# Scores of the last 16 keys computed once for all heads, ahead of the attention steps

## The chip, the cores and the metric

The kernel runs on one core of a Trainium2 chip. The metric is the device time of one execution in microseconds. The core has TensorE (matrix products into PSUM), VectorE, ScalarE, GpSimd and SyncE (which here only issues transfers); each works through its own list of instructions in order, and they meet through semaphores. All data are 32-bit floats.

## The reference, cut to what matters

The reference is one step of a decoder layer: a normalised input of 528 prompt tokens (16 learned meta tokens and 512 others) and 8 sample tokens, one combined input projection, four mixers side by side (differential attention, retention, a gated recurrence, gated linear attention), gates and a merge, an output projection, and a mixture of experts. The change touches the prompt part of the attention:

```python
def diff_attn_block(q, k, v, q_pos, k_pos, lam):
    s = jnp.einsum('bqhmd,bkhmd->bhmqk', q, k)
    s = jnp.where(k_pos[None, :] <= q_pos[:, None], s, -jnp.inf)
    p = jax.nn.softmax(s, axis=-1)
    w = p[:, :, 0] - lam * p[:, :, 1]
    return jnp.einsum('bhqk,bkhv->bqhv', w.astype(v.dtype), v)
```

There are 4 heads `h`, and each has two maps `m` of width 32; the weights of a head are the difference of its two softmax maps.

## The kernel before, in words

TensorE computes the input projection tile by tile (`tiled`, `values_tile`): a tile is 128 output columns for all tokens, and it is made in two halves of about 3.7 us. The work of the mixers is laid between these halves: `beside(name, 0)` runs between the halves of tile `name`, and `beside(name, 1)` behind it. Each engine has a `beside` of its own or a loop in the same order. The order is written out by hand in the table `ATTN`: BK0 (behind) has step 0, BK1 1 and 2, BG0 3 and 4, BG1 5 and 6, V2 7 and 8, V3 9 and 10, CX0 11 and 12, CX1 13 and 14, CG0 15 and 16, CG1 17.

An attention step `s` belongs to a head and a block `i` of 128 queries: `head_block(s)` gives `(s // 8 * 2 + s % 2, s % 8 // 2)`. Queries of block `i` see 16 + 128 (i + 1) keys, so steps 6, 7, 14 and 15 (i = 3) have 528 keys. One PSUM bank holds 512 columns. The stages of a step are:

- `scores(s)` on TensorE (L681): for both maps the product into bank 4 + m, and for i = 3 the last 16 keys into bank 7 at column 256 + 16 m.
- `causal_max(s)` on VectorE (L1816 to L1824): it adds the mask in PSUM, takes the maximum, and for i = 3 does both for the last keys too and takes the smaller of the negated maxima (L1824).
- `exps(s)` on ScalarE (L1399, and L1403 for the last keys): exponentials with their sums, into `prb` in SBUF.
- `combine(s)` on VectorE (L1834 to L1838): the weights of the head, in `prb`; it ends with `scomb`.
- `transposes(s)` on TensorE (L699) into bank 6, and for i = 3 the fifth block into bank 7; `wt_copy(s)` on ScalarE (L1412, L1415) copies them to SBUF.
- `weighted(p)` on TensorE (L714): the output product of the step pair 2p and 2p + 1, into bank 7 at column 384; `av_copy(p)` on ScalarE (L1420) copies it.

`attention_step(s)` normally issues `weighted` (at odd s), `scores(s)` and `transposes(s - 1)`. Before the change the transposes of steps 6 and 14 are not issued in steps 7 and 15 but at the start of steps 8 and 16, and three waits keep bank 7 in order: the scores of a 528-key step wait for the output copy, and `weighted` and `transposes` wait for the exponentials of the last keys (`sexp`).

VectorE's list between these stages holds a rotation in steps 6, 8, 10 and 12 (`ROTATE`, L1844 to L1846) and key reductions of the sample attention (`K_BESIDE`, L1866), one in step 6, none in step 7, one each in 8, 14, 15 and 16. The products for these reductions are GpSimd's units (L2556); each of the first 15 waits for `scomb` at the step in `K_STEP`: unit 5 for the weights of step 6, unit 10 for those of step 14. SyncE loads the key pages for them in turn with the weight tiles of the projection.

Ahead of step 0, between the halves of BK0, TensorE transposes the sample columns of queries and keys (L801) into bank 4; ScalarE copies them (L1439) and sends them to a scratch in HBM, from which SyncE broadcasts them for GpSimd. Step 0 waits for that copy (`t8_ev`).

## Time and profile before

| | |
|---|---|
| median of 3 runs | 810.36 us (809.93 to 811.4) |
| the profiled execution's own time | 807.98 us |
| its span | 806.1 us, 14317 instructions |
| TensorE busy | 767.2 us |
| VectorE busy | 381.6 us |
| ScalarE busy | 223.3 us |
| GpSimd busy | 294.8 us |

The span is the time from the first to the last instruction of the profiled execution. Busy times of the engines overlap. L12 is line 12 of the kernel. A product of 32-bit floats is recorded as two matmul records (two passes), so a step with four products shows as x8. Where an instruction has waited, the idle time before it and the instruction that ended it stand in brackets.

### The profile page before, as it was taken

The page shows a single profiled execution, that of the slowest core. Times are in us where ns is not written, and L with a number is a line of the kernel's source. Part 1 is how long each engine was busy: PE and PEld are TensorE (multiplying, and loading weights), DVE is VectorE, ACT ScalarE, POOL GpSimd, SP SyncE. Part 2 cuts the span into 40 slices and gives each one's busy share as a digit, 9 for nine tenths or more (in the row PEclk, how much of TensorE's full clock was granted, in tenths as well). Part 3 has the DMA queues.
Part 4 walks back from the last instruction along what each step waited for, and adds up shares of the span by engine and source line. Part 5 has one row for each costly group of instructions (what it writes and reads, how often), then busy time and mean ns, then how long its engine had stood idle before and what let it go on. Part 6 is the DMA issues. An engine that isn't in the chain of part 4 may idle for free.

```text
span 806.1 us, 14317 instructions
## 1 busy us (share of the span) xinstructions
PE 767.2 (95%) x5269; PEld 549.3 (68%) x5269; DVE 381.6 (47%) x729; ACT 223.3 (28%) x432; POOL 294.8 (37%) x221
## 2 busy tenths in 40 slices
PE   9999999989999999999999999999999799999992
PEld 7887777666667878777777787888888544333330
DVE  4672586867469669653542211744433632030210
ACT  4231433331413535214413222521211521020100
POOL 0000422244653975335444554524332031333214
PEclk9999999999999999999999999999999999999997
DMA  9242842244654542155543454261580889999943
GB/s 365 106 156 84 241 140 80 89 137 155 170 188 162 184 142 92 37 162 170 170 146 96 154 170 158 65 223 69 201 320 1 311 289 411 378 387 373 381 149 49
DMA packets 72538, 148.32 MB, mean 184 GB/s; under 512 B 13335, under 2 KB 47144, under 8 KB 70420
## 3 DMA queue, kind: packets, MB, share of 16 engines
q1 hardware_dynamic: 65716, 135.43, 48.1%
q0 software_dynamic: 5920, 10.82, 5.3%
q10 hardware_dynamic: 832, 1.16, 0.6%
q8 instruction: 42, 0.69, 0.3%
q14 instruction: 28, 0.23, 0.1%
HBM read 137.71 MB, written 18.90 MB: 194 GB/s over the span
## 4 chain that ended last, share of the span: by engine, by line
PE 79%; DVE 10%; ACT 3%; DMA 2%; issue 2%; SPq 2%; ACTq 0%; POOL 0%; POOLq 0%; DVEq 0%
PE ps L879 18%; PE ps L606 13%; PE ps L1212 10%; PE ps L848 6%; PE ps L1120 6%; PE ps L1282 4%; PE ps L621 3%; PE ps L649 3%; PE ps L905 2%; PE ps L681 1%; PE ps L1201 1%; PE ps L595 1%; DMA out_y<-cst,gtab 1%; SPq L432 1%; PE ps L952 1%
## 5 line engine op out<-in xcount | busy, mean ns | idle before, releaser
L606 PE MATMUL ps<-xn,ring 128*128 128x268 f32 (+1 forms) x576 | 136.7, 392 | 0.2 <-ACT qk L1375 0.2
L606 PEld LDWEIGHTS ps<-xn,ring 128*128 128x128 f32 x576 | 106.9, 190 | 24.6 <-issue 3.9
L2556 POOL TENSOR_TENSOR kv<-kv,sgd 128x1024 f32<-128x1024 f32 (+1 forms) x32 | 79.8, 2507 | 114.4 <-DVE tmp L1838 64.7
L1532 ACT ACTIVATE sgt<-sgt,vec 128x260 f32<-128x260 f32 x60 | 30.1, 510 | 129.1 <-DVE sgt L2111 77.9
L2671 POOL DMA_INDIRECT out_y<-cst,gtab x24 | 37.3, 1555 | 74.6 <-DMA out_y<-cst,gtab 35.4
L848 PE MATMUL ps<-br,ring 128*128 128x260 f32 x256 | 61.2, 386 | 0.8 <-DVE sgt L2115 0.8
L879 PE MATMUL ps<-xn,ring 128*128 128x260 f32 x240 | 58.0, 384 | 1.0 <-ACT tmp L1375 1.0
L879 PE MATMUL ps<-xn,qb 128*128 128x260 f32 x240 | 57.6, 383 | 1.1 <-DVE sgt L2112 1.1
L848 PEld LDWEIGHTS ps<-br,ring 128*128 128x128 f32 x256 | 47.8, 190 | 11.8 <-issue 3.7
L879 PEld LDWEIGHTS ps<-xn,qb 128*128 128x128 f32 x240 | 45.4, 190 | 8.4 <-issue 1.4
L879 PEld LDWEIGHTS ps<-xn,ring 128*128 128x128 f32 x240 | 45.0, 190 | 8.3 <-issue 1.4
L1866 DVE TENSOR_REDUCE sgd<-kv 128x32 f32<-128x1024 f32 (+1 forms) x32 | 40.7, 1280 | 14.5 <-POOL kv L2556 14.5
L2468 DVE TENSOR_TENSOR ring<-ring,ps 128x256 f32<-128x256 f32 x12 | 5.1, 421 | 71.1 <-ACT ring L1691 69.9
L2102 DVE TENSOR_TENSOR sgt<-ps,sgt 128x260 f32<-128x260 f32 x15 | 6.4, 427 | 64.2 <-PE ps L879 64.2
L2600 POOL TENSOR_TENSOR qb<-qb,ring 128x512 f32<-128x512 f32 x15 | 19.3, 1287 | 41.2 <-PE ps L879 41.2
L2595 POOL TENSOR_TENSOR qb<-ring 128x512 f32<-128x512 f32 x15 | 20.5, 1364 | 36.6 <-PE ps L879 36.3
L2567 POOL TENSOR_TENSOR cst<-sgt,cst 128x520 f32<-128x520 f32 x16 | 20.6, 1289 | 30.6 <-ACTq L1542 30.6
L621 PE MATMUL ps<-kv,ring 128*128 128x268 f32 x128 | 29.8, 391 | 0.2 <-DVE kv L1751 0.2
L2607 POOL TENSOR_TENSOR qb<-ring,qb 128x512 f32<-128x512 f32 x15 | 19.3, 1287 | 28.9 <-PE ps L879 28.3
L649 PE MATMUL ps<-ring,xn 128*128 128x128 f32 x256 | 29.8, 276 | 0.0
L1375 ACT ACTIVATE cst<-ps 128x520 f32<-128x520 f32 x32 | 19.3, 603 | 37.5 <-PE ps L848 37.5
L649 PEld LDWEIGHTS ps<-ring,xn 128*128 128x128 f32 x256 | 29.1, 192 | 0.5 <-ACT tmp L1375 0.3
(516 smaller groups left out, 1505.6 us busy)
## 6 DMA issues: line engine op xcount, KB each, us to landing
ring<-in_w_mg SPq DMA_DIRECT2D x32, 640.0 KB, 4.6
kv<-in_kc SPq DMA_DIRECT2D x128, 128.0 KB, 2.1
kv<-in_vc SPq DMA_DIRECT2D x128, 128.0 KB, 2.1
ring<-in_w_in SPq DMA_DIRECT2D x24, 512.0 KB, 4.8
kv<-in_w SPq DMA_DIRECT2D x8, 1024.0 KB
br<-in_w SPq DMA_DIRECT2D x7, 1024.0 KB
sgd<-in_w SPq DMA_DIRECT2D x6, 1024.0 KB, 13.9
qk<-in_w SPq DMA_DIRECT2D x6, 1024.0 KB
```

Source lines behind the costliest of these rows:

```text
L606: mm = pe.matmul(ps[:, 2 * (t % 2) + h, 0:hw], wsl(c, k), xnv[:, k, col0 + h * hw:col0 + (h + 1) * hw], start=(k == 0), stop=(k == KT - 1))
L621: mm = pe.matmul(ps[:, EARLY[name] + h, 0:HT], wsl(c, k), xgv[:, k, h * HT:(h + 1) * HT], start=(k == 0), stop=(k == KT - 1))
L649: pe.matmul(ps[:, 2 * (t % 2), b * P:(b + 1) * P], xnv[:, k, b * P:(b + 1) * P], wsl(c, k), start=(k == 0), stop=(k == KT - 1))
L848: mm = pe.matmul(ps[:, bk + h, 0:HN], wsl(CAT[f"G{n}{m}"], KT + k), brv[:, BR[n] + k, h * HN:(h + 1) * HN], start=(k == 0), stop=(k == 1))
L879: mm = pe.matmul(ps[:, bk, 0:HN], w[:, k * P:(k + 1) * P], x, start=(k == 0), stop=(k == 3))
L1120: mm = pe.matmul(ps[:, bk, 0:HN], wk, x, start=(k == 0 and i in (1, 2, 5)), stop=(k == 3), skip_group_check=(i in (6, 7, 4, 3)))
L1212: mm = pe.matmul(ps[rows, i % ROUNDS, :], xeT[i % (2 * ROUNDS)][:, k, rows], slot[(i // ROUNDS * 12 + k - k % 2 + g // 2) % STREAM][2 * (g ...
L1282: mm = pe.matmul(ps[rows, LAST_OUT[r][n] if last else 6 + n, :], hT[r][:, f, rows], w[g][2 * f + n], start=(f == 0), stop=(f == 1), tile_p ...
L1532: act.activation(g, g, ACT.Sigmoid, bias=vv(V_BM + 8 * "ABCD".index(n) + m + i)).then_inc(g_a, 1)
L1866: dve.tensor_reduce(row, kb.rearrange("p s (m d) -> p s m d", d=32), X, ALU.add).then_inc(k_used, 1)
L2556: pool.tensor_tensor(kb, kb, qbc[:, b:b + 1, :].to_broadcast([P, HALF // 2 + (half and u), 256]), ALU.mult)\
L2671: pool.indirect_dma_start(out=o["y"], out_offset=on_rows(to), in_=rows.rearrange("p a n -> p (a n)"), in_offset=None, bounds_check=N - 1, ...
```

## The change

The scores of the last 16 keys are needed by the last query block of each head and map only. They are now computed once, for all 8 maps, between the halves of BK0: eight products into banks 4 to 7, columns 0 to 31, one bank for each group of 32 rows. VectorE (`last_keys`) adds the mask, writes them into `last_s` in SBUF and keeps their negated maxima in `last_m`. The sample transposes move to columns 256 to 511 of banks 4 and 5, and ScalarE's copy waits for VectorE's masking; step 0 waits for both. The steps with 528 keys compute 512 columns of scores, take one maximum in PSUM and combine it with `last_m`, and exponentiate the last keys from SBUF. The waits around bank 7 go, the first map's exponentials no longer wait for the second map's maximum, and the transposes of steps 6 and 14 stand in steps 7 and 15, behind the scores, like those of all other steps.

The pieces are, in order: the view, TensorE's `scores`, `transposes`, `weighted`, `attention_step` and `beside`, ScalarE's `exps` and `beside`, VectorE's `causal_max` and the new `last_keys`. ScalarE's `attention_step` has the same edit for `wt_copy` as TensorE's has for `transposes`.

```diff
+        last_s, last_m = view(sgt, 600, 4, 2, META), view(sgt, 600 + 8 * META, 4, 2)
...
             def scores(s):
...
-                if n > 512:
-                    pe.wait_ge(sav_ev, (s - 1) // 2)
+                k = min(n, 512)
                 for m in range(2):
                     r = slice(32 * ((2 * h + m) % 4), 32 * ((2 * h + m) % 4) + 32)
-                    for a, b, bk, at in ((0, min(n, 512), 4 + m, 0), (512, n, 7, 256 + META * m)):
-                        if a < b:
-                            if bk == 7 and m:
-                                pe.wait_ge(sco, 2 * s + 1)
-                            mm = pe.matmul(ps[:, bk, at:at + b - a], aqk[r, h // 2, META + P * i:META + P * (i + 1)],
-                                           aqk[r, 2 + h // 2, a:b], start=True, stop=True)
-                    mm.then_inc(sco, 1)
+                    pe.matmul(ps[:, 4 + m, 0:k], aqk[r, h // 2, META + P * i:META + P * (i + 1)], aqk[r, 2 + h // 2, 0:k],
+                              start=True, stop=True).then_inc(sco, 1)
...
             def transposes(s):
...
                 if i == 3:
                     pe.wait_ge(sav_ev, s // 2)
-                    pe.wait_ge(sexp, 4 * (s // 2) + 4)
...
             def weighted(p):
...
-                if i == 2:
-                    pe.wait_ge(sexp, 4 * p + 6)
...
             def attention_step(s):
-                if s in (8, 16):
-                    transposes(s - 2)
                 if 0 <= s < 16:
                     if s == 0:
-                        pe.wait_ge(t8_ev, 1)
+                        pe.wait_ge(t8_ev, 2)
                     scores(s)
-                if 1 <= s < 17 and s not in (7, 15):
+                if 1 <= s < 17:
                     transposes(s - 1)
...
                 if (name, end) == ("BK0", 0):
                     pe.wait_ge(a_ok, 4)
+                    for j in range(2):
+                        for g in range(4):
+                            r = slice(32 * g, 32 * g + 32)
+                            pe.matmul(ps[:, 4 + g, META * j:META * (j + 1)], aqk[r, j, L - P:L], aqk[r, 2 + j, 4 * P:L], start=True, stop=True)
                     for i in range(4):
-                        mm = pe.transpose(ps[0:DEC, 4, i * P:(i + 1) * P], aqk[:, i, L:T], ident)
+                        mm = pe.transpose(ps[0:DEC, 4 + i // 2, 256 + i % 2 * P:256 + (i % 2 + 1) * P], aqk[:, i, L:T], ident)
...
                 for m in range(2):
-                    act.wait_ge(smx, 2 * s + (2 if i == 3 else m + 1))
+                    act.wait_ge(smx, 2 * s + m + 1)
...
-                        ins = act.activation(prb[:, s % 2, m, 512:n], ps[:, 7, c0:c0 + META], ACT.Exp, bias=nb,
+                        ins = act.activation(prb[:, s % 2, m, 512:n], last_s[:, (2 * h + m) % 4, h // 2, :], ACT.Exp, bias=nb,
...
                 if (name, end) == ("BK0", 0):
                     act.wait_ge(t8, 1)
-                    link(act.activation(qk8, ps[0:DEC, 4, :], ACT.Copy))
+                    act.wait_ge(t8_ev, 1)
+                    link(act.activation(fold(qk8, 256), ps[0:DEC, 4:6, 256:512], ACT.Copy))
...
                     else:
-                        dve.wait_ge(sco, 2 * s + 2)
-                        link(tt(last, last, cc(C_MASK + P, META), ALU.add))
-                        dve.tensor_reduce(sc[:, 38:39], main, X, ALU.max, negate=True)
-                        link(dve.tensor_reduce(sc[:, 39:40], last, X, ALU.max, negate=True))
-                        tt(nb, sc[:, 38:39], sc[:, 39:40], ALU.min).then_inc(smx, 1)
+                        link(dve.tensor_reduce(sc[:, 38:39], main, X, ALU.max, negate=True))
+                        tt(nb, sc[:, 38:39], last_m[:, (2 * h + m) % 4, h // 2:h // 2 + 1], ALU.min).then_inc(smx, 1)
...
+            def last_keys():
+
+                dve.wait_ge(t8, 1)
+                link(tt(last_s, ps[:, 4:8, 0:2 * META].rearrange("p g (j k) -> p g j k", j=2),
+                        cc(C_MASK + P, META).unsqueeze(1).unsqueeze(1).to_broadcast([P, 4, 2, META]), ALU.add))
+                dve.sem_inc(t8_ev, 1)
+                link(dve.tensor_reduce(last_m, last_s, X, ALU.max, negate=True))
+
+            last_keys()
             at_k = 0
             for s in range(18):
```

## Rows read from the trace of the kernel before

**Rows 1.** The page: busy us, share of the span and instructions, by engine.

```profile
PE 767.2 (95%) x5269; PEld 549.3 (68%) x5269; DVE 381.6 (47%) x729; ACT 223.3 (28%) x432; POOL 294.8 (37%) x221
```

**Rows 2.** One stretch: busy PE, PEld, DVE, ACT, POOL; PEclk, DMA share, GB/s.

```profile
215.00:320.00 105.00, 103.45 (x586) 81.92 (x585) 77.75 (x91) 41.65 (x57) 62.79 (x51) 1.00 0.50 158
```

**Rows 3.** TensorE's timeline, steps 5 to 9: start, duration, instructions, [idle before].

```profile
105.93 0.94 PE L681 MATMUL ps<-qk 32*128 32x400 f32 x4
...
111.00 1.70 PE L681 MATMUL ps<-qk 32*128 32x512 f32 x8
112.63 0.66 PE L699 MATMUL ps<-cst,tmp 128*128 128x128 f32 x4
...
117.62 1.24 PE L714 MATMUL ps<-tmp,vtok 128*64 128x128 f32 x16 [0.76 <-ACT tmp L1403]
119.32 1.67 PE L681 MATMUL ps<-qk 32*128 32x512 f32 x8 [0.47 <-ACT br L1420]
120.92 3.84 PE L649 MATMUL ps<-ring,xn 128*128 128x128 f32 x32
124.69 0.65 PE L655 MATMUL ps<-ring,xn 128*32 128x128 f32 x16
126.56 0.74 PE L699 MATMUL ps<-cst,tmp 128*128 128x128 f32 x5 [1.22 <-ACT tmp L1403]
...
128.39 0.77 PE L699 MATMUL ps<-cst,tmp 128*128 128x128 f32 x5 [0.65 <-DVE tmp L1838]
128.99 3.74 PE L649 MATMUL ps<-ring,xn 128*128 128x128 f32 x32
...
134.05 0.52 PE L681 MATMUL ps<-qk 32*128 32x144 f32 x4
```

**Rows 4.** VectorE's timeline, steps 6 and 7.

```profile
112.29 0.30 DVE L1816 TENSOR_TENSOR ps<-ps,cst 128x128 f32<-128x128 f32 x1 [0.84 <-PE ps L681]
112.81 0.18 DVE L1821 TENSOR_TENSOR ps<-ps,cst 128x16 f32<-128x16 f32 x1 [0.22 <-PE ps L681]
...
113.63 0.16 DVE L1823 TENSOR_REDUCE small<-ps 128x1 f32<-128x16 f32 x1
...
115.33 0.71 DVE L1844 TENSOR_TENSOR qb<-qb,cst 128x536 f32<-128x536 f32 x1
...
118.60 0.15 DVE L1834 TENSOR_TENSOR small<-small 128x2 f32<-128x2 f32 x1
...
119.71 0.77 DVE L1838 SCALAR_TENSOR_TENSOR tmp<-tmp,small 128x528 f32<-128x528 f32 x1
...
122.12 0.81 DVE L1824 TENSOR_TENSOR small<-small 128x1 f32<-128x1 f32 x1
```

**Rows 5.** ScalarE's timeline, the exponentials of step 7.

```profile
124.45 0.69 ACT L1399 ACTIVATE tmp<-ps,small 128x512 f32<-128x512 f32 x1 [5.28 <-DVE small L1824]
...
126.04 0.28 ACT L1403 ACTIVATE tmp<-ps,small 128x16 f32<-128x16 f32 x1
```

**Rows 6.** GpSimd's timeline, its unit beside step 7.

```profile
120.56 2.36 POOL L2556 TENSOR_TENSOR kv<-kv,sgd 128x1024 f32<-128x1024 f32 x1 [12.86 <-DVE tmp L1838]
```

**Rows 7.** TensorE's timeline, steps 14 to 17.

```profile
161.78 1.70 PE L681 MATMUL ps<-qk 32*128 32x512 f32 x8
...
176.69 0.74 PE L699 MATMUL ps<-cst,tmp 128*128 128x128 f32 x5 [1.10 <-ACT tmp L1403]
178.52 0.77 PE L699 MATMUL ps<-cst,tmp 128*128 128x128 f32 x5 [1.10 <-DVE tmp L1838]
179.12 3.78 PE L606 MATMUL ps<-xn,ring 128*128 128x268 f32 x16
```

**Rows 8.** TensorE's timeline, the first attention step.

```profile
80.98 0.51 PE L681 MATMUL ps<-qk 32*128 32x144 f32 x4
```

**Rows 9.** ScalarE's timeline, the copy ahead of the steps.

```profile
77.47 0.59 ACT L1439 ACTIVATE sgt<-ps 8x512 f32<-8x512 f32 x1 [3.43 <-PE ps L801]
```

**Rows 10.** VectorE's timeline, an update at 231 us.

```profile
231.61 3.94 DVE L1915 TENSOR_TENSOR qk<-qk,qb 128x1072 f32<-128x1072 f32 x1
```

More of the change, by code:

```diff
@@ L1401, in exps @@
                     if i == 3:
-                        c0 = 256 + META * m
-                        ins = act.activation(prb[:, s % 2, m, 512:n], ps[:, 7, c0:c0 + META], ACT.Exp, bias=nb,
+                        ins = act.activation(prb[:, s % 2, m, 512:n], last_s[:, (2 * h + m) % 4, h // 2, :], ACT.Exp, bias=nb,
                                              accum_out=sc[:, 36 + m:37 + m])
@@ L1425, in attention_step @@
                     av_copy((s - 3) // 2)
-                if s in (8, 16):
-                    wt_copy(s - 2)
-                if 1 <= s < 17 and s not in (7, 15):
+                if 1 <= s < 17:
                     wt_copy(s - 1)
@@ L1814, in causal_max @@
                     k = min(n, 512)
-                    last = ps[:, 7, 256 + META * m:256 + META * (m + 1)]
                     link(tt(main[:, n - 144:k], main[:, n - 144:k], cc(C_MASK, k - n + 144), ALU.add))
```

## The prediction

> **What bounds the kernel now.** I began with the page: TensorE is busy for 95% of the span [rows 1]. Then came the busy times by stretch. Behind the attention steps, from 215 to 320 us, TensorE works 103.45 of 105 us at a granted clock of 1.00 [rows 2], so work or waiting taken from TensorE earlier moves all that follows forward. Last I read the timelines of the engines around the four steps with 528 keys. Steps 5 to 13 otherwise run as a tight alternation of half tiles and attention pieces; around steps 6 to 8 TensorE stands still four times [rows 3], and around 14 to 16 again [rows 7]. The reader is to see who ends each wait: ScalarE with the exponentials of the last keys (L1403), ScalarE with the output copy, and VectorE with the weights (L1838).
>
> **Work taken off TensorE.** Per 528-key step the sixteen-column products go. A step with 144 columns takes 0.52 us and one with 400 takes 0.94, so 512 would take 0.94 + 112 x 0.42/256 = 1.12 us; the row with 512 + 16 shows 1.70 [rows 3]. That is 0.58 us a step for four narrow passes, 0.145 each, and 2.3 us for four steps. Start to start, a bare step is then 1.63 - 0.58, about 1.06 us (111.00 to 112.63).
>
> **Work put ahead.** The same scores for all eight maps are 8 products of two passes, 16 passes. At 0.145 they cost 2.3 us, which is the upper bound; the lower is nothing, if the four groups of 32 rows run side by side and under the weight loads. The 0.145 contains the pause between the two maps. Also, the two maps of a step use different row groups and overlap: a column costs 0.42/256/4 = 0.41 ns a pass there, but 3.78/16/268 = 0.88 ns in a half tile of 128 rows [rows 7]. So I take half of the upper bound, 1.1 us. The Trainium skill (TensorE: Matmul & The Clock Gate, "Why this matters for your kernels") says that products of 32 rows in separate row groups run concurrently, with a gain of 3.07 for four at 512 columns; 16 x 0.145 / 3.07 gives an estimate of 0.8 us and a sum 0.3 us lower. No row shows four at once.
>
> **What hides the rest of the preparation.** VectorE now masks 128 columns, then ScalarE copies the sample rows, and TensorE waits for both before step 0. ScalarE's copy began at 77.47 and took 0.59; step 0 came at 80.98 [rows 8, 9], after a half tile. The cover is 80.98 - 78.06 = 2.9 us against a handover of some 0.6 us (a masking near 0.3 and two signals): nothing is paid, and if the half tile did not lie between, the masking's 0.6 would be added to the copy's wait. The scratch transfer of sample queries leaves 1.1 + 0.6 = 1.7 us later, and with it SyncE's broadcast, its key-page loads queued behind, and GpSimd's first unit. Those units wait for later steps' weights anyway, so SyncE and GpSimd have caught up by the third. The maxima of the last keys (eight columns) run on VectorE before it waits for step 0. I price all of this at 0.
>
> **Steps 6 to 8, replayed.** Times are those of before; the 1.1 us is added at the end. Step 6's scores start at 111.00 and end at 112.06; transposes of step 5 take 0.49, to 112.55; V2's first half takes 3.7 (the 3.74 of the row less the overlap), to 116.2. Before, the output product then stood until 117.62, because the last keys lay in its bank. That wait is gone: the product runs 117.62 less 1.4, from 116.2, and its 16 passes at 1.17 end at 117.4. The wait for the output copy is gone too: step 7's scores run to 118.5. Now the transposes of step 6 come here, and not behind V2's second half.
>
> They need VectorE's weights of step 6. Before, the two maxima took 112.29 to 115.33, rotation and one key reduction to 118.60, and the weights to 120.48 [rows 4]. Each map loses the mask of 0.18 and the maximum of 0.16 with their handovers, 0.37 us; with 0.13 for the earlier start that puts the weights at 120.48 - 0.87 = 119.6. The transposes start at 119.7, with **a new wait of 1.2 us**. Behind it in TensorE's order stand V2's second half and all later tiles. The transposes take 0.6, to 120.3, the half with its tail of 24 rows 4.35 (120.92 to 124.69, and 0.65 less the overlap), to 124.65. Step 8's scores end at 125.1.
>
> Then the transposes of step 7. The two maxima of step 7 can start at 119.7 and would take 2.3 us. But GpSimd starts a unit when step 6's weights are done: 120.56 and 2.36 us before [rows 6], 119.7 to 122.05 now. The tiny minimum at L1824 shows what that does: started at 122.12 it took 0.81, ending as the unit ends at 122.92, against 0.16 alone. The Trainium skill (SBUF — State Buffer, "SBUF: two separate sides") names it: a VectorE operation with two SBUF inputs and a GpSimd operation that reads SBUF exclude each other for a whole instruction; by that rule, the trace agrees, the new minimum is caught earlier in the unit. It would be reached at 120.8 and ends at 122.1. So the second map's maximum is there at 123.35, not 122.0. A pair of exponentials takes 0.93 (124.45 to 126.32 for two) [rows 5]: the second ends at 124.4, and the weights, 1.88 long, at 126.3. The transposes start at 126.35, **a new wait of 1.25 us**, and V3 starts at 126.95 against 128.99: 2.0 us gained. Without the exclusion it is 3.0; if each min were held a full unit it is about 1.
>
> **Steps 14 to 16, replayed.** No rotation stands there. Scores 161.78 to 162.84, transposes 0.49, half tile 3.7: 167.04. Output product 168.2, step 15's scores 169.3. Step 14's maxima end at 165.25, the key reduction at 166.4, the weights at 168.3, so its transposes find them ready: 169.9. CG0's second half takes 3.8, to 173.7. The maxima of step 15 start at 169.4, and the first minimum is held 0.3 us by the unit that step 14's weights release (168.4 to 170.75); maxima end 172.0, key reduction 173.15, weights 175.05. The transposes start at 175.1, **a wait of 1.4 us**, and CG1 starts at 175.7 against 179.12 [rows 7]: 3.4 us gained.
>
> **The sum.** -2.0 - 3.4 + 1.1 = -4.35 us with the unrounded terms. Checked the other way: 2.3 us of products and the waits of both groups, some 7.1 us start to start, go; 1.1 of products and 3.85 of waits come. Against the profiled execution's own 807.98 us (span 806.1 and 1.9 around it) that is 803.6; this execution lies 2.4 under the median of the runs, 810.36, which becomes 806.0. Of no change a measurement here can tell about 0.2%, 1.6 us.
>
> **What carries it to the end.** The wait of step 11's transposes for the last rotation is untouched and moves along. GpSimd's key units, SyncE's page loads and the retention steps are released by TensorE's tiles or by these weights, so they shift too. One place is delicate: at 231.61 VectorE spent 3.94 us on an update of 1072 elements with two inputs in SBUF [rows 10], beside a GpSimd unit, and VectorE's chain from there to 252 us leads into TensorE's key states. GpSimd's units there follow page loads, not TensorE, so their phase may move by a microsecond.
>
> **Rivals.**
> - *The exclusion costs nothing or the passes overlap fully.* If the minimum falls outside the unit, 1.3 us more; if the 16 passes are hidden, 1.1 more. Up to -6.3, typically -5.6: 804.8. For it: in step 14's maxima no unit runs. Against: the unit is released by the very weights after which step 7's maxima start. 14%.
> - *The gain is given back near 231 us.* Another update in that chain meets a unit: for up to the unit's 2.36 us [rows 6]. -4.35 + 2.36 = -2.0: 808.4. For it: one seems held already. Against: both engines start from shifted events. 13%, half of it still beyond 0.2%.
> - *The edits shift the waits only* (no change). If step 6's and 14's transposes each wait 2.2 us more than replayed, all is used up: 810.4. 4%.
> - *Slower: the moved transposes hold the half tiles.* Before, a half tile lay between scores and transposes and covered VectorE's 3.3 us of rotation and reduction (115.33 to 118.60). Now only the output product and scores, 2.2 us, do. Each microsecond by which these weights come later than 119.6 and 168.3 is TensorE's. It decides from 3 us late in both: -4.35 + 6 = +1.65, 812.0. For it: VectorE's chain already ends last there. Against: with shorter maxima it ends earlier than before, and ScalarE's exponentials end before VectorE is through with the rotation. 4%.
> - My forecast has the remaining 65%.
>
> **Numbers.** Faster is 65 + 14 + 6 (about half of the second rival) = 85%, same 7 + 4 = 11%, slower 4%. The range: low end from the first rival's full size with the median's scatter, 810.36 - 6.3 - 0.5 = 803.6; high end the second rival, 808.4, with 0.6 of scatter, 809.0. Under 2 in 10 lie outside. The likeliest alone spans 804.8 to 807.6.
>
> **What would show it.** In the changed profile: narrow passes once ahead of step 0, near 1.1 us, and 1.1 us score rows in steps 6, 7, 14 and 15; no wait at the output products of these steps; a wait near 1.2 before the transposes between step 7's scores and V2's second half, released by VectorE; none at step 14's; about 1.3 before step 7's and step 15's; a minimum of 1.3 us in step 7. Step 0 should begin 1.1 us later, V3 about 0.9 earlier, CG1 about 4.3 earlier, and the first merge products the same 4.3. The prediction is wrong if the first new wait exceeds 3 us, if the granted clock leaves 1.00 before 620 us, or if a wait appears at the key states near 250 us that was not there.

## The result and the profile after

The changed kernel takes 802.15 us (median of 6 executions, 800.97 to 803.06), the kernel before beside it 809.53 (6, 808.45 to 811.4). The ratio is 0.9913, 95% interval 0.9898 to 0.9928. The sign was foreseen, the time was not: 806.0 was forecast, and 802.15 lies 1.45 us below the range's low end, 803.6. The profiled execution took 802.6 us with a span of 800.7, against 807.98 and 806.1 before: 5.4 less in each.

The page answers to [rows 1]: TensorE's busy time hardly changes (767.2 to 766.7), the span shrinks around it.

```profile
PE 766.7 (96%) x5269; PEld 547.8 (68%) x5269; DVE 380.7 (48%) x715; ACT 224.6 (28%) x432; POOL 294.5 (37%) x221
```

TensorE's timeline of after, ahead of the steps: the narrow passes (L793), the sample transposes, BK0's second half, step 0. Start, duration, instructions.

```profile
77.11 0.63 PE L793 MATMUL ps<-qk 32*128 32x16 f32 x16
77.67 0.60 PE L795 MATMUL ps<-cst,qk 128*8 128x128 f32 x4
78.11 3.78 PE L607 MATMUL ps<-xn,ring 128*128 128x268 f32 x16
81.81 0.52 PE L677 MATMUL ps<-qk 32*128 32x144 f32 x4
```

From start to start the sixteen passes take 0.56 us, 0.035 each, where the prediction had 1.1. Step 0 begins 0.83 later than before [rows 8]. Of this, 0.27 is not the passes: 0.18 stands there already at 66 us, ahead of everything that the change touches, and two traces of one kernel differ by 0.1 to 0.2 there.

TensorE's timeline of after, steps 6 to 9, against [rows 3]:

```profile
111.61 1.13 PE L677 MATMUL ps<-qk 32*128 32x512 f32 x4
112.67 0.66 PE L693 MATMUL ps<-cst,tmp 128*128 128x128 f32 x4
113.17 3.74 PE L650 MATMUL ps<-ring,xn 128*128 128x128 f32 x32
116.83 1.24 PE L706 MATMUL ps<-tmp,vtok 128*64 128x128 f32 x16
118.00 1.13 PE L677 MATMUL ps<-qk 32*128 32x512 f32 x4
120.23 0.77 PE L693 MATMUL ps<-cst,tmp 128*128 128x128 f32 x5 [1.10 <-DVE tmp L1826]
120.83 3.74 PE L650 MATMUL ps<-ring,xn 128*128 128x128 f32 x32
...
126.83 0.77 PE L693 MATMUL ps<-cst,tmp 128*128 128x128 f32 x5 [1.24 <-DVE tmp L1826]
127.43 3.74 PE L650 MATMUL ps<-ring,xn 128*128 128x128 f32 x32
```

The four waits of before are gone; two new ones stand in their place, both ended by VectorE's weights, 1.10 where 1.2 was forecast and 1.24 where 1.25 was. V3 begins at 127.43, 1.56 earlier than before. VectorE in step 7, and the GpSimd unit of that moment:

```profile
119.41 0.77 DVE L1826 SCALAR_TENSOR_TENSOR tmp<-tmp,small 128x528 f32<-128x528 f32 x1
120.09 0.29 DVE L1807 TENSOR_TENSOR ps<-ps,cst 128x128 f32<-128x128 f32 x1
120.42 0.69 DVE L1811 TENSOR_REDUCE small<-ps 128x1 f32<-128x512 f32 x1
121.14 1.49 DVE L1812 TENSOR_TENSOR small<-small,sgt 128x1 f32<-128x1 f32 x1
```

```profile
120.25 2.36 POOL L2553 TENSOR_TENSOR kv<-kv,sgd 128x1024 f32<-128x1024 f32 x1 [11.95 <-DVE tmp L1826]
```

The minimum of one element takes 1.49 us and ends as the unit does (120.25 + 2.36 = 122.61); with no unit beside it, at 113.83, it takes 0.16. That is the hold which the prediction placed here.

TensorE's timeline of after, steps 14 to 17, against [rows 7]:

```profile
160.22 1.13 PE L677 MATMUL ps<-qk 32*128 32x512 f32 x4
...
167.71 0.77 PE L693 MATMUL ps<-cst,tmp 128*128 128x128 f32 x5
168.31 3.78 PE L607 MATMUL ps<-xn,ring 128*128 128x268 f32 x16
173.41 0.77 PE L693 MATMUL ps<-cst,tmp 128*128 128x128 f32 x5 [1.31 <-DVE tmp L1826]
174.01 3.78 PE L607 MATMUL ps<-xn,ring 128*128 128x268 f32 x16
```

No wait at step 14's transposes, 1.31 at step 15's (1.4 forecast), and CG1 begins at 174.01 against 179.12: 5.11 us earlier, where 4.35 was forecast. From there to about 400 us every instruction of TensorE is 5.1 to 5.2 us earlier. Two windows follow: the stretch of [rows 2], as full as before, and one at 402 us that the prediction had not. In a window, PEclk is the clock that TensorE was granted, as a share of its full one; it is the third number from the end.

```profile
215.00:320.00 105.00, 103.54 (x596) 82.74 (x595) 82.10 (x96) 41.01 (x55) 61.49 (x52) 1.00 0.49 152
402.00:415.00 13.00, 12.62 (x212) 10.40 (x211) 6.96 (x16) 1.60 (x4) 4.61 (x3) 0.87 0.58 178
```

The granted clock is 0.87 there. In TensorE's timeline one group of eight passes takes 3.67 us, where the same shape takes 1.92 next to it:

```profile
404.22 1.92 PE L873 MATMUL ps<-xn,qb 128*128 128x260 f32 x8
...
408.50 3.67 PE L873 MATMUL ps<-xn,ring 128*128 128x260 f32 x8
```

That costs 1.7 us. A stretch of this kind is called "at half clock" below. TensorE was at the lower of its two levels (1.2 instead of 2.4 GHz), after work that had kept it nearly full: only the 0.38 us before L974 stand idle.

### The profile page after: what moved, and what is told of

Read it like the earlier page. It is cut to its first block, busy times and chain, and to the rows that moved or that the text cites. A ratio compares the mean times of both kernels' runs of the same rounds, so it can differ in the third digit from the quotient of the medians.

```text
span 800.7 us, 14290 instructions
## 1 busy us (share of the span) xinstructions
PE 766.7 (96%) x5269; PEld 547.8 (68%) x5269; DVE 380.7 (48%) x715; ACT 224.6 (28%) x432; POOL 294.5 (37%) x221
## 3 DMA queue, kind: packets, MB, share of 16 engines
q10 hardware_dynamic: 832, 1.16, 0.6%
## 4 chain that ended last, share of the span: by engine, by line
PE 83%; DVE 10%; DMA 2%; ACT 2%; issue 1%; POOL 0%; SPq 0%; POOLq 0%; ACTq 0%; DVEq 0%
PE ps L873 20%; PE ps L607 14%; PE ps L1206 10%; PE ps L842 7%; PE ps L1114 6%; PE ps L1276 4%; PE ps L622 3%; PE ps L650 3%; PE ps L899 2%; PE ps L1195 1%; PE ps L596 1%; DMA out_y<-cst,gtab 1%; PE ps L677 1%; DMA tmp<-in_xT 1%; PE ps L946 1%
```

## The experiments

Each kernel was timed beside the kernel before on the same chip. "V3" and "CG1" are the starts of these tiles in the trace, right behind the transposes of steps 7 and 15; in after they are 127.43 and 174.01.

### Both kernels again, on another chip

No edit in either.

> The kernel before, unchanged, once more. The profiled pair differs by 5.3 us (806.1 to 800.7) in span, the medians by 7.4 us (809.53 to 802.15). Theory A: the profiled execution of before, 807.98 us, was a quick one of its kind and executions scatter by 1 to 2 us; then this ratio is 1.000 within 0.15% and its profiled span lies nearer 807.5. Rival B: before has a loss of 1.5 us to 2 us in most executions that its first profile did not catch; then this profile shows that loss in one place, as a wait of TensorE that the first one lacks.

> The changed kernel, unchanged, once more. Theory A (scatter): the ratio to before is nearer the 5.3 us of the profiles, 0.9930 to 0.9935. Rival B (a real gain beyond the attention steps): 0.9905 to 0.9915 again, some 7.3 us.

Before again: 807.93 us (12 executions, 805.09 to 808.83), ratio 0.9998 (0.9986 to 1.001). The kernel before beside it: 807.74 (17, 805.97 to 811.42). After again: 802.44 (6, 801.31 to 803.07), ratio 0.9922 (0.9902 to 0.9941). So the time of after repeats within 0.3 us. The ratio lies between the two expectations and settles neither. Before had medians of 809.53, 807.74, 808.34, 808.84 and 809.06 over the five groups of runs of this study. The 810.36 of three executions, on which the prediction built, is the highest of all; the median of all 68 executions of before on record is 808.45, that of the 12 of after 802.30.

The second trace of before had a span of 803.2, not near 807.5 as theory A said: it was the quicker of the two, and no loss showed that the first had missed. It runs as the first to 484 us, 0.2 earlier. There the first one waited for a transfer, and the second did not (TensorE's timelines of before, then of before again):

```profile
484.33 1.48 PE L905 MATMUL ps<-kv,cst 128*4 128x256 f32 x24
486.90 1.03 PE L905 MATMUL ps<-kv,cst 128*4 128x256 f32 x10 [1.09 <-DMA kv<-scr_v]
```

```profile
484.13 2.32 PE L905 MATMUL ps<-kv,cst 128*4 128x256 f32 x34
```

The wait costs 1.3 us. Another 0.5 comes near 645 us, where every kernel here has a stretch at half clock (granted clock 0.89 from 630 to 660 us in both) that does not always fall on the same instructions, and 0.9 comes behind TensorE's last product. Two executions of one kernel can thus differ by 3 us without any edit.

The gain in the stretch that was edited does not scatter like that. In the two new traces CG1 begins at 179.05 and 174.11, 4.94 us apart, against 5.11 in the first two. The second trace of after has no half clock at 408 us (granted clock 1.00 from 405 to 415 us) but has it at 254 us instead (0.57 from 254 to 258), and loses 1.6 us there. So its place is not a property of the kernel.

### The transposes back in the old order

Like after, but the transposes and copies of steps 6 and 14 stand at the start of steps 8 and 16 again.

```diff
 def attention_step(s):            # TensorE; ScalarE's wt_copy likewise
+    if s in (8, 16):
+        transposes(s - 2)
...
-    if 1 <= s < 17:
+    if 1 <= s < 17 and s not in (7, 15):
         transposes(s - 1)
```

> The changed kernel with the transposes of steps 6 and 14, and their copies, back at the start of steps 8 and 16; the narrow products stay ahead and the waits around bank 7 stay gone. Theory (the chain from VectorE's maxima of steps 7 and 15 over ScalarE's exponentials to VectorE's weights ends last in both orders): V3 and CG1 start within 0.2 us of the changed kernel's 127.43 and 174.01, the time is the same within 0.3 us; the wait before V2's second half goes and comes back behind it. Rival (the new place of the transposes is itself worth the 1.1 us waits it replaces, as the prediction's replay suggests when read stage by stage): 1 to 2.4 us slower than the changed kernel.

Measured: 803.05 us (802.14 to 803.56), ratio 0.9931 (0.9911 to 0.995). TensorE's timeline of this kernel:

```profile
123.56 0.76 PE L693 MATMUL ps<-cst,tmp 128*128 128x128 f32 x5
125.04 0.51 PE L677 MATMUL ps<-qk 32*128 32x144 f32 x4 [0.72 <-ACT tmp L1398]
126.97 0.77 PE L693 MATMUL ps<-cst,tmp 128*128 128x128 f32 x5 [1.41 <-DVE tmp L1830]
127.57 5.36 PE L650 MATMUL ps<-ring,xn 128*128 128x128 f32 x32
```

V3 begins at 127.57, 0.14 from after. Step 14 to CG1 takes 13.78 (161.98 to 175.76), in after 13.79. The waits differ (0.72 and 1.41 here, 1.10 and 1.24 there), the length of both groups does not; the 0.14 stands there already before step 6. The move in itself is worth nothing either way; the gain is that of the shorter scores and the removed waits. The 5.36 of a half tile that takes 3.74 elsewhere is again a stretch at half clock: from 120 to 135 us this kernel's granted clock is 0.89, after's 1.00. It follows the waits, and accounts for 1.6 of this trace's later 1.75 us at CG1.

```profile
120.00:135.00 15.00, 12.87 (x117) 11.40 (x116) 10.85 (x25) 5.13 (x19) 4.70 (x2) 0.89 0.25 70
```

### The minimum as a scalar operation

The per-partition value of the last keys enters as a scalar operand, so VectorE reads one tensor from SBUF and not two.

```diff
-tt(nb, sc[:, 38:39], last_m[...], ALU.min).then_inc(smx, 1)
+ts(nb, sc[:, 38:39], last_m[...], None, ALU.min).then_inc(smx, 1)
```

> The changed kernel with the minimum of step maxima written as a tensor-scalar operation with the last keys' maximum as its per-partition scalar, so it has one tensor input instead of two. Theory (a VectorE operation with two tensor inputs in SBUF is held until GpSimd's unit ends): the 1.49 us of the minimum in step 7 falls to 0.16, the wait before step 7's transposes from 1.24 to about 0.3, V3 starts 1.0 us earlier, step 15 gives 0.2 more: 1.1 us faster than the changed kernel. Rival (the hold does not depend on the number of tensor inputs, or the scalar form is held as well): 1.49 us stays, no change.

Measured: 800.31 us (799.49 to 801.89), ratio 0.9902 (0.9882 to 0.9922). VectorE's timeline, step 7:

```profile
120.57 0.69 DVE L1811 TENSOR_REDUCE small<-ps 128x1 f32<-128x512 f32 x1
121.29 0.21 DVE L1812 TENSOR_SCALAR small<-small,sgt 128x1 f32<-128x1 f32 x1
```

0.21 us instead of 1.49 at the same moment beside the same unit. The wait before step 7's transposes is gone, V3 starts at 126.41 and CG1 at 172.92. So the hold cost TensorE 1.0 to 1.1 us. The median lies 2.1 under that of after on the same chip; the traces give the reason for 1.1 of that only, and the trace of after has a stretch at half clock (1.7 us) that this one has not. The Trainium skill (SBUF — State Buffer, "Who interferes with whom") says that only a VectorE instruction with two SBUF inputs, or one in a two-port mode, contends with GpSimd, and lists tensor_scalar among those that can enter such a mode; this form of one element did not contend.

### The GpSimd unit later

Unit 5 waits for step 7's weights, not step 6's.

```diff
-K_STEP = [1, 2, 3, 4, 5, 7,
+K_STEP = [1, 2, 3, 4, 5, 8,
```

> The changed kernel with GpSimd's unit 5 released by the weights of step 7 and not of step 6. Theory (the unit holds whichever two-input operation of VectorE meets it): the minimum in step 7 takes 0.16 us, not 1.49, and V3 starts 1.0 us earlier; the unit then runs beside step 8, where the first rotation operation is held by about 1.2 us, and the transposes of step 8 may wait up to 1.0 us for their weights. Net gain at CG1 0 to 0.6 us. Rival (the minimum was slow for another reason): it stays at 1.49.

Measured: 801.23 us (800.81 to 801.34), ratio 0.9918 (0.9895 to 0.9941). The minimum takes 0.16, and V3 starts at 126.27, 1.16 earlier. The hold moved to the next operation of two SBUF inputs. VectorE's timeline in step 8, and GpSimd's:

```profile
126.77 1.86 DVE L1832 TENSOR_TENSOR qb<-qb,cst 128x536 f32<-128x536 f32 x1
```

```profile
125.69 2.37 POOL L2553 TENSOR_TENSOR kv<-kv,sgd 128x1024 f32<-128x1024 f32 x1 [17.37 <-DVE tmp L1826]
```

The first piece of the rotation takes 1.86 instead of 0.71 and ends 0.57 behind the unit (128.63 against 128.06), as if it began its work only then; step 8's transposes then wait 0.48, and of the 1.16 about 0.6 is left at CG1 (173.40). Moving the unit only chooses its victim; changing the operand form removes it.

### Twice the narrow passes

```diff
-for j in range(2):
+for j in (0, 1, 0, 1):
```

> The changed kernel with the eight narrow products issued twice, so 32 passes. Theory (passes on four row groups run side by side; the changed kernel's 16 took 0.56 us, 0.035 each): the half tile behind them and every later mark, CG1's start too, come 0.56 us later. Rival (the prediction's 1.1 us, or 0.145 a pass as in the steps): 1.1 or 2.3 us later.

Measured: 801.76 us (801.3 to 802.59), ratio 0.9925 (0.99 to 0.9949). The 32 passes take 1.02 us from start to start (76.87 to 77.89), so 16 more cost 0.46. TensorE's timeline there:

```profile
76.87 1.08 PE L793 MATMUL ps<-qk 32*128 32x16 f32 x32
77.89 0.60 PE L795 MATMUL ps<-cst,qk 128*8 128x128 f32 x4
```

The price of 0.03 to 0.035 us a pass holds. CG1 starts 0.53 later, near the 0.56 expected, but partly by luck. This trace begins the passes 0.24 earlier than after's, so step 6 comes only 0.22 later (111.83). The other 0.31 is the rest of a stretch at half clock behind 121 us (granted clock 0.83 from 118 to 128), which the wait ahead of step 7's transposes took up for the most part.

The figure of the Trainium skill (TensorE: Matmul & The Clock Gate, "Why this matters for your kernels") gave an estimate of 0.8 us for the 16 passes of after. The row that I halved gave 1.1. Both were too dear: 0.56 was measured.

### Late weights

Two fills of 1072 columns on VectorE (about 1.9 us) ahead of the weights of steps 6 and 14. They write a part that nothing reads at that time.

```diff
+if s in (6, 14):
+    for _ in range(2):
+        link(dve.memset(hold, 0.0))
 if s < 16:
     combine(s)
```

> The changed kernel with two fills of 1072 unused columns, about 1.9 us together, on VectorE ahead of the weights of steps 6 and 14. Theory (the prediction's slower rival as a mechanism: with the transposes ahead of the half tile every microsecond of the weights is TensorE's): V3 starts 1.9 us later; around step 14 the slack of 1.0 us ahead of its transposes takes part, but step 15's chain is pushed through the held minimum, so CG1 comes 3.0 to 3.8 us later. Rival (the half tiles' slack covers it): under 1 us later.

Measured: 808.11 us (10 executions, from 805.9; one took 2019.58 and hardly moves the median), ratio 0.9994 (0.9978 to 1.001): the whole gain is gone. TensorE's timeline:

```profile
122.69 1.21 PE L694 MATMUL ps<-cst,tmp 128*128 128x128 f32 x5 [3.60 <-DVE tmp L1827]
123.68 4.98 PE L651 MATMUL ps<-ring,xn 128*128 128x128 f32 x32
```

The wait grows from 1.10 to 3.60. Then come transposes of 1.21 instead of 0.77 and a half tile of 4.98 instead of 3.74, at half clock. V3 starts 2.79 later, CG1 5.17 later; 3.0 to 3.8 was expected. The weights of step 6 come 2.45 later than in after, since the fills are 0.95 each and VectorE stands idle ahead of each. TensorE passes this on in full. The stretch at half clock lost 1.68 us (0.44 and 1.24), but most of it fell before a wait: step 7's weights end at 129.23, and its transposes start at 129.61, so some 0.3 of it is left at V3. Steps 14 to CG1 take 16.18 instead of 13.79, 2.39 more. So the 5.17 is lateness of the weights twice, with about 0.3 from the clock, and nearly each microsecond of it is TensorE's, as the fourth rival said. The expectation had counted 1.9 us for each pair of fills, where the weights moved by about 2.4, and no half clock.

### The bank wait back

The scores of a 528-key step wait for the output copy again.

```diff
+if n > 512:
+    pe.wait_ge(sav_ev, (s - 1) // 2)
```

> The changed kernel with the scores of the 528-key steps waiting again for the output copy, as before the change. Theory (in step 7 VectorE still has the weights of step 6 to finish, so later scores cost nothing; in step 15 the scores start its chain): V3 unchanged within 0.1 us, CG1 0.5 us later. Rival (the 0.5 us wait counts wherever it stands): 1.0 us later.

Measured: 801.57 us (800.94 to 801.74), ratio 0.9919 (0.9896 to 0.9943). The wait of 0.47 comes back twice. In step 7 it displaces waiting that was there anyway: the transposes of step 6 wait 0.56 instead of 1.10. V3 starts 0.19 later, and not 0.1 at most, because a stretch at half clock lies behind 120 us (granted clock 0.83 from 118 to 128). In step 15 step 14's transposes had no such slack: step 14 to CG1 takes 14.13 instead of 13.79, 0.34 more, and CG1 starts 0.52 later. The median, 801.57, is even below that of after, so an edit of this size shows in the trace alone.

### The key reduction one step later, alone and with the scalar minimum

VectorE's reduction of step 6 (1.21 us, between the maxima and the weights) moves to step 7, where VectorE stands idle 1.13 us for ScalarE.

```diff
-K_BESIDE = [0, 0, 1, 1, 1, 1, 1, 0, 1,
+K_BESIDE = [0, 0, 1, 1, 1, 1, 0, 1, 1,
```

> The changed kernel, with VectorE's key reduction of step 6 (1.21 us at 117.17 in the trace of after) moved to step 7, where VectorE stands idle 1.13 us for ScalarE's last exponentials. My account of the wait before step 6's transposes (1.10 us): VectorE gives the weights too late because this reduction lies between the maxima and the weights. By it, combine of step 6 starts 1.1 earlier, the wait goes, and V2's second half begins near 119.7 instead of 120.83. In step 7 the minimum then runs at about 120.1, just ahead of the GpSimd unit, so it may take 0.16 instead of 1.49; the weights come near 125.0 for transposes due at 124.5, so that wait shrinks from 1.24 to about 0.5. V3 starts 1.1 to 1.9 us earlier than in after (I take 1.7), the group of steps 12 to 15 is unchanged, time near 800.5. Rival: the exponentials of ScalarE (end 116.2) or the rotation, not the reduction, set the weights: then V3 moves by less than 0.3 and the time stays near 802.2. Second rival: the reduction in step 7 delays step 7's weights by as much: V3 moves by 0 to 0.5.

> The changed kernel with two edits together: the minimum as a scalar operation (alone it brought V3 forward by 1.02 us and CG1 by 1.09) and the key reduction of step 6 moved to step 7. The first removes step 7's wait of 1.24, the second step 6's wait of 1.10; with both, V3 can start at most 2.34 us earlier than in after (127.43). Step 7's weights then come near 125.0 for transposes due at 124.5, so a wait of 0.4 to 0.6 remains and I expect V3 1.7 to 2.0 earlier, CG1 the same plus 0.1, time 800.0. Rival: the two are one and the same wait counted twice (if the reduction moves the minimum out of the unit's way, nothing is left for the scalar form): then this is equal to the kernel with the moved reduction alone, within 0.3 us in the trace.

Alone: 799.97 us (799.68 to 801.96), ratio 0.9902 (0.9882 to 0.9923). The wait before step 6's transposes is gone as expected (they start at 119.19). But the unit is released earlier by the same weights, so the minimum is held 1.29 again and step 7's wait stays at 1.26. V3 starts at 126.41: 1.02 earlier, not the 1.7 that I took. With the scalar minimum as well: 799.28 us (798.13 to 801.13), ratio 0.9892 (0.9872 to 0.9912). Both waits are gone, and TensorE runs steps 6 to 9 without standing still:

```profile
118.03 1.13 PE L677 MATMUL ps<-qk 32*128 32x512 f32 x4
119.24 0.77 PE L693 MATMUL ps<-cst,tmp 128*128 128x128 f32 x5
119.84 3.74 PE L650 MATMUL ps<-ring,xn 128*128 128x128 f32 x32
...
124.72 0.77 PE L693 MATMUL ps<-cst,tmp 128*128 128x128 f32 x5
125.32 3.74 PE L650 MATMUL ps<-ring,xn 128*128 128x128 f32 x32
```

V3 starts 2.11 earlier than in after: 1.02 from one edit, 1.09 from the other. They are two waits, not one counted twice. The medians, 799.28 and 799.97, are too near each other to show it; the traces do.

### Step 15 in another order, and its key reduction

Both edits as above, and in step 15 the scores ahead of the weighted sums, the exponentials ahead of the copy of step 14's weights, and the weights ahead of the key reduction.

```diff
 def attention_step(s):                    # TensorE
+    if s == 15:
+        scores(s)
     if s >= 3 and s % 2:
         weighted((s - 3) // 2)
...
 def attention_step(s):                    # ScalarE, behind av_copy
+    if s == 15:
+        exps(s)
     if 1 <= s < 17:
         wt_copy(s - 1)
...
-at_k = sampled(at_k, K_BESIDE[s])         # VectorE
+if s != 15:
+    at_k = sampled(at_k, K_BESIDE[s])
 if s < 16:
     combine(s)
+if s == 15:
+    at_k = sampled(at_k, K_BESIDE[s])
```

> As the kernel with both edits, and in step 15 a third: TensorE issues the scores ahead of the weighted sums of the pair before (1.17 us earlier), ScalarE issues the exponentials ahead of its copy of step 14's weights, and VectorE makes the weights ahead of its key reduction. In after, step 15's transposes wait 1.31 us for a chain scores, maxima, copy, exponentials, weights. With it that chain starts 1.17 earlier and loses the copy's 0.75 and the reduction's place, so the wait before step 15's transposes goes; but step 14's transposes, which stand right behind the weighted sums, now wait for ScalarE's copy of them out of the bank they share, about 0.5. Net at CG1: 0.6 to 0.9 earlier than with the two edits alone, time near 799.3. Rival: ScalarE's output copy stands ahead of the exponentials and waits for the weighted sums, so the exponentials start no earlier and the wait of 1.15 stays, with the new 0.5 on top: CG1 0.4 later than with the two edits alone, time 800.5.

At CG1 the expectation held: 171.02 against 171.83 with two edits, no wait before step 15's transposes, and 0.47 before step 14's. The time did not: 804.03 us (8 executions, 798.66 to 806.8), ratio 0.9929 (0.9903 to 0.9956). TensorE's timeline of this kernel near 250 us, and its granted clock there:

```profile
247.76 5.26 PE L771 MATMUL ps<-vtok,tmp 128*64 128x64 f32 x40 [2.34 <-DVE tmp L1955]
```

```profile
247.00:263.00 16.00, 15.24 (x144) 11.05 (x145) 12.11 (x14) 4.82 (x7) 9.83 (x7) 0.57 0.70 230
```

With two edits, the same group:

```profile
245.72 3.52 PE L769 MATMUL ps<-vtok,tmp 128*64 128x64 f32 x40 [0.46 <-DVE tmp L1948]
```

A wait of 2.34 us instead of 0.46, then a stretch at half clock. The group that begins at 260.30 with two edits begins at 268.40 here, 8.1 us later, and what follows stays so. From CG1 on it has lost 8.9 us: 2.85 by the start of the state products (1.88 of them in that wait, 0.50 in a new wait for VectorE at 232 us), and 6.1 at half clock behind them.

This is the trace of the slowest of its eight executions, at a mean granted clock of 0.981. Five took 803.62 to 806.8 us, at clocks of 0.980 to 0.986, and three took 798.66 to 800.78, at 0.988 to 0.990. So the loss comes in some executions of this kernel and not in others, and only one with it was traced.

The last kernel differs from this one in one point: the key reduction of step 15 stands ahead of the weights again.

> As the kernel with the third edit (step 15: scores ahead of the weighted sums, exponentials ahead of the copy), but VectorE's key reduction of step 15 stays where the two-edit kernel has it, ahead of the weights. In the three-edit kernel CG1 began 0.81 us earlier than with two edits, and then TensorE waited 2.34 us (0.46 with two) for VectorE before the state products at 247.8, and ran the next stretch at a granted clock of 0.52 (250 to 263 us). My account: the reduction put behind the weights freed its key buffer later, the GpSimd unit's load landed later, and VectorE, which works in order, was held near 231 to 242 us. VectorE has 1.13 us idle ahead of step 15's weights and the reduction takes 1.21, so step 15's weights lose 0.1 and CG1 keeps its gain of 0.8 over two edits. By it the wait before the state products is 0.4 to 0.6 again, no half-clock stretch near 250 us, span 795.2 to 795.8, time 798.5. Rival: the earlier group itself brings the key chain and its loads out of step, wherever the reduction stands: then the wait before the state products is again over 1.5, and the time 800 to 804. Second rival: the half-clock stretch comes there by chance and without that wait: then its place moves or it vanishes while the wait stays at 2.3.

Measured: 798.19 us (4 executions, 797.52 to 799.55), ratio 0.9872 (0.9856 to 0.9888), the fastest kernel of the study. The wait before the state products is 0.5 again, there is no half clock near 250 us, and CG1 starts at 170.76, 1.07 earlier than with two edits.

```profile
244.65 3.52 PE L771 MATMUL ps<-vtok,tmp 128*64 128x64 f32 x40 [0.47 <-DVE tmp L1952]
```

This speaks for the place of one reduction of 1.21 us in step 15 as what brought the loss of some 6 us in, 75 us later, and against the earlier group. It does not settle it: none of four executions lost here, where five of eight did there, and if the two kernels were alike that would still come about once in 14 times.

The traces show how the lateness travelled. In the kernel that lost, VectorE's three key reductions ahead of the state products began at 242.40 instead of 240.35. In the chain before them an update of two SBUF tensors met a GpSimd unit (232.81 to 235.16). VectorE, first in the kernel that lost, then with two edits:

```profile
233.43 2.86 DVE L1900 TENSOR_TENSOR qk<-qk,qb 128x1072 f32<-128x1072 f32 x1
```

```profile
232.91 1.34 DVE L1893 TENSOR_TENSOR qk<-qk,qb 128x1072 f32<-128x1072 f32 x1
```

It took 1.52 longer and began 0.52 later, together 2.04 of the 2.05. That is the mechanism of the prediction's second rival. GpSimd's units there follow page loads; that the reduction's new place shifted them was not tested by an edit of its own.

## Why the prediction was right or wrong

**The replay was right.** Each wait that it named is in the trace at its place and near its size: 1.10, 1.24 and 1.31 where 1.2, 1.25 and 1.4 were forecast, none at step 14's transposes, and no wait at the output products. The group around steps 6 to 8 gained 2.17 (2.04 forecast), that around 14 to 16 3.55 (3.42). The reasons held as well: the hold at the minimum (scalar form), lateness of the weights (late weights), the bank wait (bank wait back).

**The step that failed: the base of the sum.** "This execution lies 2.4 under the median of the runs, 810.36, which becomes 806.0." The 810.36 is the median of three executions, and it stood for the kernel's own time. All 68 executions of before have a median of 808.45, so 1.9 of the 3.85 us missed lies in this base. The range inherited the fault, since its low end was also counted from 810.36: from 808.45 it would have begun at 801.65. Counted by the one pair of traces the base looks worse still (2.38 between profile and median of before, 0.45 the other way in after, 2.83 together), but that sum holds the scatter of two single executions. The range had a slip besides: 4.35, 1.3 and 1.1 add up to 6.75, not to the 6.3 used. That would have put its low end at 803.1, still above 802.15.

**The gain was too small as well.** It was forecast at 4.35. The first pair of traces shows 5.4, the medians of all executions 6.15.

**The terms of the sum that were mis-sized.** They make most of the 1.0 us between the forecast and the traces:

- *The narrow passes:* 1.1 forecast, 0.56 measured, confirmed by doubling them. The upper bound of 0.145 a pass came from a row that held a pause, and I took half of it; the truth was a quarter of it. 0.54.
- *Absorbed lateness:* the delay was added at the end, as if nothing ahead of step 6 stood still. It begins 0.61 later, not 0.83; a gap of step 2 took 0.22.
- *The two groups:* 0.13 more each, 0.26 together.

They sum to 1.02; against them stand 0.27 of start variation, for 0.75 at CG1: 5.11 instead of 4.35. From there the pair of traces moved by events far behind the edited stretch, of nearly equal size both ways: after lost 1.7 to the half clock at 408 us, before lost 1.25 to the transfer at 486 us and 0.6 near 645 us, a net 0.2.

**The rivals.** The first came in part: the passes cost half of what was forecast, the minimum was held in full. Its price, 804.8, suffers from the same base. The second did not come in after: the chain near 231 us was no worse. But its mechanism is what the trace of the kernel with the third edit shows. No change: no. Slower: no, but its price is real. Weights some 2.4 us later in both places cost 5.17 at CG1, of which about 0.3 is the clock's. That is the two times 2.4 by which this rival counts, and it agrees with the third rival's 2.2 each as the point at which the forecast gain of 4.35 is used up.

**A condition missed.** That the granted clock leaves 1.00 before 620 us was named as a sign of error, and it did, at 408 us. It did not carry the error, being worth 1.7 in the other direction.

**What stays open.** The traces give 5.2 us to 400 us; the medians differ by 5.3 to 7.4, depending on the group of runs, and by 6.15 over all. Part of the rest seems to go with TensorE's clock. Over the 62 executions of before whose clock is on record, the mean granted clock is 0.9858; over the 12 of after it is 0.9877. Both traces of before are of executions with an unusually high one (0.989 and 0.990; ten of the 62 are at 0.989 or above). Among before's own executions the nine at 0.983 have a median of 809.5 and the six at 0.990 one of 806.2, so 0.001 goes with some 0.5 us, and the difference of 0.0019 with some 0.9 (an estimate from these medians). That is about the size of what the first pair of traces leaves unexplained, 0.8. It is a correlation: no trace shows which stretches the slower executions of before had. Nor did I settle whether waits for a transfer like that at 486 us are more frequent before.

Nor is it known what places the short stretches at half clock. Near 120 and 127 us they follow waits of 0.56 to 3.60 us, but after has a wait of 1.10 at the same place and no such stretch; at 408 us there is only one of 0.38; and two executions of after have it at different places.

## What to carry to other kernels

Replay the stretch around the edit engine by engine. That gives the gain, and it held here within 0.8 us. The base it is taken from needs its own care: a median of three executions stood 1.9 above that of 68, and one profiled execution 0.5 below it. Take more executions, or give the range this much on both sides.

When a wait is moved, look for what the engine that now ends last does between its input and its output. Here one reduction and one operand form were worth 2.1 us with no work saved, and they could be read from after's timeline.

Before a small piece is placed where it "costs nothing", follow whom it releases. The same 1.21 us reduction on one side of the weights and on the other went with medians of 804.03 (eight executions, three of them at 801 or below) and 798.19 (four).

## What the runs showed of the hardware

- Passes of 16 columns with 32 rows, spread over four row groups, take 0.035 us each (16 in 0.56, 32 in 1.02), against 0.145 in the row with two groups and a pause.
- A one-element minimum of two SBUF tensors is held until the GpSimd unit beside it ends (1.49 and 1.29 us, 0.16 alone); the same minimum with one of them as a scalar operand is not (0.21). Delaying the unit moves the hold to the next operation of that kind (1.86 instead of 0.71).
- TensorE falls to half clock for single half tiles (5.36 for 3.74 us) in a kernel that keeps it 96% busy. The places differ from kernel to kernel, and between two executions of one (after at 408 and at 254 us). Each such stretch costs 1.6 to 1.7 us if nothing behind it was waiting anyway; in three kernels (narrow passes twice, late weights, bank wait) it lay before a wait, and about 0.3 was left. Behind a wait of 2.34 us one lasted from 248 to some 262 us and cost 6.1.
- Executions of one kernel on one chip differ by up to 8 us, and the time goes with the mean granted clock: in the kernel with the third edit from 798.66 at 0.990 to 806.8 at 0.981.
